# One 128-byte tensor ahead of the shared operand space in a two-block transformer kernel

## The chip, the core and the metric

The program runs on one NeuronCore of a Trainium2 chip. The metric is the device time of one execution in microseconds. The core has five engines with queues of their own: TensorE (PE, with its weight loads shown apart as PEld), VectorE (DVE), ScalarE (ACT), GpSimd (POOL) and SyncE (SP, which here only issues transfers).

## What is computed

Two blocks of two layers each work on x of 512 tokens by 2048 channels, in fp32. Each layer normalises x, multiplies it by a wide input matrix, mixes (gated linear attention and forgetting attention; a state space layer; a linear recurrent unit and window attention; latent attention and differential attention), gates, and multiplies by an output matrix:

```python
h = rms_norm(x, norm_g)
z = h @ w_in                     # 2048 x (4096 to 7200)
...                              # mixing and gates
return x + mixed @ w_out         # 2048 x 2048
```

The result is the normalised x after the fourth layer. The weight products are nearly all of the arithmetic.

## The kernel before

**Products.** Each large product runs in phases (the list PHASES), each phase in regions, blocks of 512 columns and pieces of 2 × 512 weights per partition. SP loads a piece into `raw` (a ring of four); ACT copies it to `whi`, rounded to fp32r (L386); DVE subtracts to make `wlo` (L392). The operand from x is split in the same way into `a_hi`, `a_lo` or `b_hi`, `b_lo`, each 16 tiles of 512 fp32r. TensorE then makes three products for each tile (L603):

```python
for n_pass, (ws, hs) in enumerate(((whi, hi), (whi, lo), (wlo, hi))):
    c = k * r.pitch
    if r.form == "T":
        lhsT = ws[:, slot, c + m * P:c + m * P + r.rows(m)]
        rhs = hs[:, kt, :]
    else:
        lhsT = hs[:, kt, m * P:(m + 1) * P]
        rhs = ws[:, slot, c:c + r.width]
```

In form "T" the weights are the stationary operand (loaded by LDWEIGHTS) and x is the moving one, 512 columns; in form "N" the roles change. Two regions have narrow stationary operands, of 24 and of 64 columns. Attention, recurrences and norms have small matmuls of their own, in plain fp32, which are put between the pieces.

**Order.** Each engine's instructions stand in a fixed order; `beside` and `mixed` deal the steps of a mixing stage out among the pieces of a product phase. Semaphores tie the engines together. L443 to L447 sum squares over the partitions with fp32 matmuls against `ones` and `eps_all`.

**Space.** `sb` places tensors one behind the other in each partition. First come those that live throughout. Everything else lies in one space behind them: `overlay(base, tensors)` lets groups of tensors share it, each group beginning `base` bytes (0, 65536 or 131072) behind the last tensor that `sb` placed. In the built program the addresses in bytes are:

```
raw    16512      acc       75744      a_hi, xa, w_p, d_ug   84864
whi    32896      eps_all   83040      r_y                   88992
wlo    49280      r_sp      84672      b_hi, xb, g_q, f_p   150400
stage  65664                           m_p                  176032
ident  73856      (r_sp is the         mx_o, glu_z          215936
ones   74368       last of sb)         s_kv ends at         228480
```

So `whi` begins at 128 modulo 256 and so does `a_hi`; from one to the other it is 51968 bytes, 203 times 256. `ones`, `ident`, `xa_acc`, `f_p` and `w_p` also are at 128 modulo 256, `acc` at 224, `eps_all` at 96, `m_p`, `m_o`, `r_y` and `r_o` at 160.

Of the kernel before, what the change touches and what calls it, by code (L numbers as in the profile page):

```python
# [127 lines left out]
def build(nc, inp, out):  # L128
    ctx = ExitStack()

    def sem(name):
        return ctx.enter_context(nc.semaphore(name))
# [4 lines left out]
    def sb(name, shape, dtype=F32):  # L137
        return ctx.enter_context(nc.sbuf_tensor(name, [P] + shape, dtype))
# [32 lines left out]
    eps_sq, eps_all, gains_two, rstd_col = sb("eps_sq", [1]), sb("eps_all", [P]), sb("gains_two", [KT]), sb("rstd_col", [NTOK])  # L171
    rows = sb("rows", [2, P])
    r_sp = sb("r_sp", [6, RB])
    ident_in = sem("identity_in")
    NCONST = len(VECTORS) + 3
    VECTORS_AFTER = 8
# [2630 lines left out]
```

## Time and profile before

| | |
|---|---|
| median of 3 runs | 3452.27 us (3450.07 to 3458.89) |
| profiled execution | 3455.26 us, its span 3453.5 us |
| mean granted TensorE clock | 0.988 |
| busy: PE, PEld | 3346.3 us (97%), 2702.4 us (78%) |
| busy: DVE, ACT, POOL | 1637.2 us (47%), 1289.0 us (37%), 520.9 us (15%) |
| moved by DMA | 525.06 MB, 152 GB/s |

The profiled execution takes 1.8 us more than its span from first to last instruction. Matmuls are pipelined: each is shown from its start to a modelled end, so that neighbours overlap; the pace of TensorE is read from one start to the next.

### The profile page before, as it was taken

The numbers are of one execution on the slowest core, as the hardware profiler recorded it, in microseconds if no ns is written. First come the engines' busy times: TensorE is split into PE (matmuls) and PEld (weight loads), VectorE is DVE, ScalarE is ACT, GpSimd is POOL, SyncE is SP. The second block draws the span as 40 slices with busy tenths as digits, with TensorE's granted clock in tenths as the row PEclk, the third lists the DMA queues.
The fourth block names the chain that finished last, engine by engine and source line by source line (L and its number), as shares of the span: only waits on it lengthen the run. The fifth ranks groups of instructions, "written<-read, shape, count | busy, mean of one in ns | idle before, by whom it ended". The sixth has DMA issues, their size and how long they took to land.

```text
span 3453.5 us, 41721 instructions
## 1 busy us (share of the span) xinstructions
PE 3346.3 (97%) x16417; PEld 2702.4 (78%) x16417; DVE 1637.2 (47%) x2691; ACT 1289.0 (37%) x1997; POOL 520.9 (15%) x754
## 2 busy tenths in 40 slices
PE   7999999999999999999999899999999999999996
PEld 6777887888888888888887676788878788777885
DVE  7895654434344444344344655543324333455532
ACT  4443433343233333433342445433223333456322
POOL 0001312323110000100331010121000111110211
PEclk9999999999999999999999999999999999999998
DMA  6776433546348776544335343453434733433631
GB/s 208 217 234 195 129 104 111 157 141 215 121 169 218 220 216 171 183 146 145 119 108 177 107 132 105 143 193 119 146 85 130 217 120 107 138 116 107 215 129 68
DMA packets 278948, 525.06 MB, mean 152 GB/s; under 512 B 64126, under 2 KB 99525, under 8 KB 273633
## 3 DMA queue, kind: packets, MB, share of 16 engines
q1 hardware_dynamic: 222352, 336.59, 32.6%
q0 software_dynamic: 54224, 182.52, 15.5%
q10 hardware_dynamic: 2176, 3.28, 0.4%
q8 instruction: 131, 2.15, 0.3%
q14 instruction: 65, 0.52, 0.0%
HBM read 408.32 MB, written 113.97 MB: 151 GB/s over the span
## 4 chain that ended last, share of the span: by engine, by line
PE 70%; DVE 4%; ACT 3%; DMA 2%; issue 2%; POOL 1%; ACTq 0%; DVEq 0%; POOLq 0%
PE pg L603 61%; PE pm L1288 2%; PE pm L1317 2%; DMA mx_g<-zt 2%; PE pm L1304 1%; PE pm L2392 1%; ACT whi L386 1%; PE pm L2396 0%; PE pm L2380 0%; DVE r_y L1673 0%; DVE d_x L2480 0%; ACT stage L481 0%; DVE xa L699 0%; ACT w_p L1353 0%; POOL mx_o L850 0%
## 5 line engine op out<-in xcount | busy, mean ns | idle before, releaser
L392 DVE TENSOR_TENSOR wlo<-raw,whi 128x1024 fp32r<-128x1024 f32 x523 | 664.3, 1275 | 1253.9 <-ACT whi L386 1253.0
L386 ACT ACTIVATE whi<-raw 128x1024 fp32r<-128x1024 f32 x523 | 548.6, 1054 | 1103.7 <-PE pg L603 1103.2
L603 PE MATMUL pg<-a_hi,whi 128*128 128x512 f32 x1856 | 744.3, 401 | 11.6 <-DVE wlo L392 4.3
L603 PE MATMUL pg<-a_hi,wlo 128*128 128x512 f32 x1856 | 727.2, 392 | 0.0
L603 PE MATMUL pg<-a_lo,whi 128*128 128x512 f32 x1856 | 726.4, 391 | 0.0
L603 PE MATMUL pg<-b_hi,whi 128*128 128x512 f32 x1568 | 618.9, 395 | 8.9 <-DVE stage L546 3.2
L603 PE MATMUL pg<-b_hi,wlo 128*128 128x512 f32 x1568 | 611.5, 390 | 0.0
L603 PE MATMUL pg<-b_lo,whi 128*128 128x512 f32 x1568 | 611.0, 390 | 0.0
L603 PEld LDWEIGHTS pg<-a_hi,whi 128*128 128x128 f32 x1856 | 348.5, 188 | 91.0 <-issue 14.3
L603 PEld LDWEIGHTS pg<-a_hi,wlo 128*128 128x128 f32 x1856 | 348.3, 188 | 77.9
L603 PEld LDWEIGHTS pg<-a_lo,whi 128*128 128x128 f32 x1856 | 348.9, 188 | 73.6 <-issue 2.6
L603 PEld LDWEIGHTS pg<-b_hi,whi 128*128 128x128 f32 x1568 | 294.8, 188 | 75.1 <-issue 6.5
L603 PEld LDWEIGHTS pg<-b_hi,wlo 128*128 128x128 f32 x1568 | 294.7, 188 | 62.4
L603 PEld LDWEIGHTS pg<-b_lo,whi 128*128 128x128 f32 x1568 | 294.8, 188 | 60.5 <-issue 1.2
L645 POOL DMA_DIRECT2D zt<-stage x144 | 78.5, 547 | 573.4 <-DVE stage L546 291.6
L603 PE MATMUL pg<-whi,a_hi 128*128 128x512 f32 x384 | 155.9, 406 | 0.0
L603 PE MATMUL pg<-wlo,a_hi 128*128 128x512 f32 x384 | 150.3, 391 | 0.0
L603 PE MATMUL pg<-whi,a_lo 128*128 128x512 f32 x384 | 149.9, 390 | 0.0
L1353 ACT ACTIVATE m_p<-m_p,m_small 128x128 f32<-128x128 f32 (+3 forms) x96 | 54.1, 563 | 211.0 <-DVE m_small L1419 210.5
L1416 DVE CUSTOM_DVE_ANT_0 m_p<-pm,wide 128x128 f32<-128x128 f32 (+3 forms) x96 | 47.1, 491 | 138.8 <-PE pm L1288 69.6
L657 POOL TENSOR_TENSOR acc<-acc,xa_sq 128x512 f32<-128x512 f32 x45 | 62.2, 1383 | 307.3 <-ACT xa_sq L505 302.1
L603 PE MATMUL pg<-whi,b_hi 128*128 128x512 f32 x256 | 101.7, 397 | 0.0
(434 smaller groups left out, 3844.8 us busy)
## 6 DMA issues: line engine op xcount, KB each, us to landing
raw<-in_l_w_in SPq DMA_DIRECT2D x169, 512.0 KB, 3.7
raw<-in_ab_w_in SPq DMA_DIRECT2D x112, 512.0 KB, 3.7
zt<-stage POOLq DMA_DIRECT2D x142, 256.0 KB, 3.6
raw<-in_c_w_in SPq DMA_DIRECT2D x64, 512.0 KB, 5.0
raw<-in_l_w_out SPq DMA_DIRECT2D x64, 512.0 KB, 3.7
raw<-in_ab_w_out SPq DMA_DIRECT2D x32, 512.0 KB, 3.7
raw<-in_glu_w SPq DMA_DIRECT2D x32, 512.0 KB, 4.4
raw<-in_c_w_out SPq DMA_DIRECT2D x32, 512.0 KB, 3.7
```

Of the source, the lines that this page charges most:

```text
L386: nc.scalar.activation(used(whi, n), used(raw, n), ACT.Copy).then_inc(hi_ready, 1)
L392: nc.vector.tensor_tensor(used(wlo, n), used(raw, n), used(whi, n).bitcast(F32), ALU.subtract).then_inc(lo_ready, 1)
L603: ins = nc.tensor.matmul(pg[m][:r.rows(m), :r.cols()], lhsT, rhs, start=(kt == 0 and n_pass == 0), stop=(kt == r.kts - 1 and n_pass == 2))
L645: pool.dma_start(r.dst(i, m, r), stage[:r.rows(m), m, :r.cols()]).then_inc(stored[m], 16)
L657: nc.gpsimd.tensor_tensor(total[:, :], total[:, :], squares[:, m % 2, :], ALU.add).then_inc(acc_done, 1)
L1288: ins = nc.tensor.matmul(pm[n % 2][:, :count * P], lhsT, rhs, start=(i == 0), stop=(i == len(ops) - 1))
L1304: ins = nc.tensor.transpose(pm[2][:, at:at + P], p[:, b * P:(b + 1) * P], ident[:, :])
L1317: ins = nc.tensor.matmul(pm[3][o * a.dv:(o + 1) * a.dv, qb * P:(qb + 1) * P], a.value(t, o, first + b), a.buf["pt"][:, n % 2, at:at + P], ...
L1353: nc.scalar.activation(p, p, ACT.Exp, bias=a.buf["small"][:, s:s + 1], accum_out=a.buf["small"][:, 4 + s:5 + s]).then_inc(att["probs"], 1)
L1416: run(vec.tensor_tensor_reduce(out=a.buf["p"][:, s, :count * P], in0=pm[n % 2][:, :count * P], in1=a.bias(t, qb, count), scale=a.scale, sc ...
L2392: nc.tensor.matmul(y_of(j), V6["d_x"][:, n, j, :, :].rearrange("p g k -> p (g k)"), V6["d_C"][:, n, j, 1:, :], start=(n == 0 and j % 4 == ...
```

## The change

One tensor of 32 floats, 128 bytes in each partition, is placed behind `r_sp`. Nothing reads or writes it. No instruction is added, removed or moved. Every tensor of `overlay` begins 128 bytes later; `raw`, `whi`, `wlo`, `stage`, `ident`, `ones`, `cols`, `acc`, `rstd` and the other tensors of `sb` stay. `a_hi` then begins at 84992, a multiple of 1024, and lies 52096 bytes behind `whi`, which is 203.5 times 256. The last byte used moves from 228480 to 228608.

```diff
@@ -171,6 +171,7 @@
     eps_sq, eps_all, gains_two, rstd_col = sb("eps_sq", [1]), sb("eps_all", [P]), sb("gains_two", [KT]), sb("rstd_col", [NTOK])
     rows = sb("rows", [2, P])
     r_sp = sb("r_sp", [6, RB])
+    sb("space_ahead_of_operands", [32])
     ident_in = sem("identity_in")
     NCONST = len(VECTORS) + 3
     VECTORS_AFTER = 8
```

## Rows read from the trace of the kernel before

**Rows 1.** The page: the span, and the chain that ended last, by engine and line.

```profile
span 3453.5 us, 41721 instructions
...
PE 70%; DVE 4%; ACT 3%; DMA 2%; issue 2%; POOL 1%; ACTq 0%; DVEq 0%; POOLq 0%
PE pg L603 61%; PE pm L1288 2%; PE pm L1317 2%; DMA mx_g<-zt 2%; PE pm L1304 1%; PE pm L2392 1%; ACT whi L386 1%; PE pm L2396 0%; PE pm L2380 0%; DVE r_y L1673 0%; DVE d_x L2480 0%; ACT stage L481 0%; DVE xa L699 0%; ACT w_p L1353 0%; POOL mx_o L850 0%
```

**Rows 2.** The page's costliest groups: the products of L603, first of three passes.

```profile
L603 PE MATMUL pg<-a_hi,whi 128*128 128x512 f32 x1856 | 744.3, 401 | 11.6 <-DVE wlo L392 4.3
...
L603 PE MATMUL pg<-b_hi,whi 128*128 128x512 f32 x1568 | 618.9, 395 | 8.9 <-DVE stage L546 3.2
...
L603 PE MATMUL pg<-whi,a_hi 128*128 128x512 f32 x384 | 155.9, 406 | 0.0
...
L603 PE MATMUL pg<-whi,b_hi 128*128 128x512 f32 x256 | 101.7, 397 | 0.0
```

**Rows 3.** Timeline, form T: start us, us, engine, what.

```profile
1650.17 0.39 PE L603 MATMUL pg<-b_hi,whi 128*128 128x512 f32 x1
1650.17 0.19 PEld L603 LDWEIGHTS pg<-b_lo,whi 128*128 128x128 f32 x1
...
1650.39 0.39 PE L603 MATMUL pg<-b_lo,whi 128*128 128x512 f32 x1
```

**Rows 4.** Chain that ended last, in order of time: start us, us, instructions.

```profile
1022.36 32.79 PE pg L603 x144
...
1064.00 16.55 PE pg L603 x72
...
1388.23 212.19 PE pg L603 x936
```

**Rows 5.** Timeline and busy table of a stretch at the lower clock.

```profile
532.28 0.63 PE L603 MATMUL pg<-whi,a_lo 128*128 128x512 f32 x1
532.71 0.63 PE L603 MATMUL pg<-wlo,a_hi 128*128 128x512 f32 x1
533.13 0.44 PE L603 MATMUL pg<-whi,a_hi 128*128 128x512 f32 x1
...
529.90:533.20 3.30, 3.19 (x12) 2.93 (x13) 2.90 (x4) 1.54 (x3) 3.21 (x3) 0.50 0.71 212
1388.00:1600.00 212.00, 212.00 (x938) 175.56 (x936) 86.19 (x97) 74.86 (x91) 29.21 (x54) 1.00 0.51 166
```

**Rows 6.** Timeline of the sums of squares, plain fp32.

```profile
1792.97 1.02 PE L443 MATMUL pm<-xa_acc,ones 128*128 128x512 f32 x2
1793.82 1.02 PE L444 MATMUL pm<-acc,eps_all 128*128 128x512 f32 x2
1794.68 1.02 PE L445 MATMUL pm<-acc,ones 128*128 128x512 f32 x2
```

**Rows 7.** Timeline of the two narrow regions, first and last of eleven and nine.

```profile
85.60 0.40 PE L603 MATMUL pg<-a_hi,wlo 128*24 128x512 f32 x1
...
87.92 0.40 PE L603 MATMUL pg<-a_hi,whi 128*24 128x512 f32 x1
...
2540.15 0.40 PE L603 MATMUL pg<-a_hi,whi 128*64 128x512 f32 x1
...
2542.00 0.39 PE L603 MATMUL pg<-a_hi,wlo 128*64 128x512 f32 x1
```

**Rows 8.** Groups of instructions, shapes apart: same shape, other addresses.

```profile
L1353 ACT ACTIVATE w_p<-w_p,w_small 128x256 f32<-128x256 f32 x48 | 24.5, 509 | 1.6
...
L1353 ACT ACTIVATE m_p<-m_p,m_small 128x256 f32<-128x256 f32 x24 | 12.2, 510 | 41.4 <-DVE m_small L1419 41.4
```

**Rows 9.** DMA issues: KB each, median us from issue to landing.

```profile
mx_g<-zt POOLq DMA_DIRECT2D x48, 256.0 KB, 4.2
...
mix<-r_o POOLq DMA_DIRECT2D x8, 256.0 KB, 2.3
...
mix<-w_o POOLq DMA_DIRECT2D x8, 256.0 KB, 2.3
```

## The prediction

> **What bounds the kernel now.** I read the chain that ended last first: TensorE holds 70% of it, L603 alone 61%, transfers 2% [rows 1]. Then the costliest groups: L603 runs 3 × (1856 + 1568 + 384 + 256) = 12,192 matmuls of 512 columns on the two operand pairs, and their idle time before is some 20 us in all [rows 2]. So TensorE is almost never starved, and what counts is its pace. The timeline gives it: a matmul starts 0.22 to 0.23 us after the one before, its weight load starts with the matmul ahead of it and is over after 0.19 us [rows 3]. Over a long stretch the pace is sharper: 936 matmuls in 212.19 us, 226.7 ns each, at the full granted clock (1.00, the 2.4 GHz level) [rows 4, 5]. 12,192 × 226.7 ns = 2764 us, 80% of the span.
>
> Within those 226.7 ns there is something to ask about. In a stretch with the granted clock at 0.50 (1.2 GHz) three starts lie 0.85 us apart, 425 ns a matmul [rows 5]. Half of that is 212.5 ns, so at the higher clock each matmul takes 226.7 - 212.5 = 14.2 ns more than a doubling of the pace would give. If those 14.2 ns came from where the operands lie, the change could touch 12,192 × 14.2 ns = 173 us.
>
> **The change, part by part.** It adds no instruction, no transfer, no wait and no semaphore, and each queue keeps its order. SP's and POOL's queues are past nothing new. What it alters is one relation: the stationary and the moving operand of L603 were both at 128 modulo 256 bytes; now the weights are there and the x operand is at 0. The work is the same, so every term is the duration of something at another address.
>
> *TensorE.* The direct row is the sums of squares: three fp32 products of 512 columns, back to back. L443 reads operands 0 bytes apart modulo 256 (`xa_acc` and `ones`), L444 operands 128 bytes apart modulo 256 (`acc` and `eps_all`), L445 96 bytes apart. They start 0.85 and 0.86 us apart and each lasts 1.02 us [rows 6]. The relation that the change makes is the one of L444, and it costs nothing there. They are plain fp32 and spend 0.85 us on 512 columns where fp32r spends 0.227, so a conflict could hide in them that shows at four times the pace. That is what stays unknown.
>
> Two more rows bear on the fp32r pace itself. In form N the operands change roles: moving is `whi` at 128 modulo 2048, stationary is `b_hi` at 896 modulo 2048 plus steps of 512; 144 matmuls take 32.79 us, 227.7 ns [rows 4]. In form T it is the other way round, at 226.7. So differences in the higher bits of the address do nothing. And where the stationary operand is only 24 or 64 columns, so that far fewer bytes of weights are read, the pace is (87.92 - 85.60)/10 = 232 ns and (2542.00 - 2540.15)/8 = 231 ns [rows 7], not less. If reads of weights stole time from the reads of the moving operand, fewer weights would steal less. The extra 14.2 ns so look like something each fp32r matmul pays at the higher clock, wherever its operands are. I take 0 us. The bounds: -173 us if all of it goes, and, as nothing excludes a loss, +173 us if as much again comes.
>
> The Trainium skill, TensorE: Matmul & The Clock Gate, section "Wait — 56ns, not 53.3ns?", gives N ÷ 2.4 GHz plus about 2.5 ns from start to start, 215.7 ns at 512 columns. The trace has 226.7 for fp32r. By the page, 12,192 × 11.0 ns = 134 us would be there to win, if layout were the cause; the page doesn't say that it is, and no run here shows it.
>
> *Contention.* Not every stretch runs at 226.7: one of 72 matmuls takes 16.55 us, 229.9 ns [rows 4], while other engines work beside it. If the new addresses removed or brought such stretching on every matmul, that would be 12,192 × 3.2 ns = 39 us either way. I take 0, as the same set of engines reads and writes the same amounts.
>
> *ACT, DVE, POOL.* Their operands move by 128 bytes too. Same work at other addresses costs the same: L1353 on 128x256 takes 509 ns on `w_p` (128 modulo 256) and 510 ns on `m_p` (160) [rows 8]. They also lie beside TensorE's work most of the time: 4% and 3% of the chain [rows 1]. Were a DVE or ACT operation on the chain 1% slower, that would be 0.07 × 3453 × 0.01 = 2.4 us. I take 0.
>
> *Transfers.* Loads of weights and stores from `stage` keep their addresses. Those into and out of the shared space move from 128 to 0 modulo 256. Stores of the same size from `w_o` (128) and `r_o` (160) land after the same 2.3 us [rows 9]. On the chain transfers are 2%, mostly `mx_g`, whose 256 KB take 4.2 us [rows 1, 9]. Were each of them 5% shorter, 0.02 × 3453 × 0.05 = 3.5 us would go; I take 0 and keep 3.5 us as the bound either way. The Trainium skill, DMA: Bandwidth & Descriptors, section "How a descriptor splits into AXI transactions", has a transfer that does not start on a multiple of 256 bytes fetch the bytes below its start too. A run of 2048 bytes that starts 128 bytes off would cost 68 beats against 64; by it an estimate is 6% off the transfers on the chain, 4 us, which is not to be seen here either.
>
> **Sum.** 0 + 0 + 0 + 0: the profiled time of 3455.3 us stays. The three runs have a median of 3452.3 us, 3.0 us below the profiled execution, so I forecast 3452 us. About what a measurement can tell from no change is 0.3%, 10.4 us; that is 10.4 us / 12,192 = 0.85 ns on each matmul.
>
> **The rivals.**
>
> *The phase of the operands is what costs the 14.2 ns* (faster). For it: both operands sit at the same place modulo 256 in both forms and in every one of the 12,192, and all show the same pace, so the trace has no fp32r matmul that would refute it. Against it: the narrow weights, and L443 to L445 [rows 6, 7]. It would give 3452 - 173 = 3279 us. By the page on TensorE the pace would fall to 215.7 ns and the time to 3452 - 134 = 3318 us; the narrow regions don't agree with what it would need. Chance 0.06.
>
> *A new conflict between the two reads* (slower, the other side). The place: TensorE's reads at L603, where the weight load lies wholly inside the matmul before it [rows 3]. If equal phases are what keeps the two reads apart, unequal ones make them meet, at up to as much as is there now: 3452 + 173 = 3625 us. It decides from 0.85 ns a matmul. For it: nothing in the trace has fp32r operands half a 256-byte unit apart. Against it: L444 is such a pair and is not slower than L443, and the weight load has 0.03 us to spare in each pace [rows 3]. Chance 0.07.
>
> *Less contention with the other engines* (faster by a part of 39 us, 3414 to 3442 us): for it, the stretches at 229.9; against it, that most of the time is at 226.7 already, so only a part of the matmuls can gain. Chance 0.08. *More of it* (slower, 3462 to 3491 us): the same rows with the other sign. Chance 0.06.
>
> *The change doesn't do what it says*: the unused tensor might get no space, and all addresses would stay. That gives 3452 us as well and belongs to the forecast's case.
>
> **How the numbers follow.** No change that can be measured 0.73; faster 0.06 + 0.08 = 0.14; slower 0.07 + 0.06 = 0.13. The forecast's own range is 3442 to 3462 us. The two small cases reach to 3414 and 3491, but their whole price needs every matmul to be touched; with about the nearer two thirds of each, 3425 to 3480 us leaves under 2 in 10 outside. The large cases stay outside.
>
> **What would show it.** The pace of L603 in the long stretch beginning near 1388 us: 212.2 us for 936 matmuls if I am right. A total of 198 to 202 us would be the faster rival, over 213 the slower. The stretches of form N should show 227 to 228 ns, where now the weights' side is moving and x is stationary; if only one form changes, it is the moving operand's address that counts and not the relation. The narrow regions should stay at 231 to 232. ACT on 128x256 should stay at 510 ns, `mx_g` at about 4.2 us. The prediction is wrong if fp32r reads at full pace see a conflict that the four times slower fp32 pairs hide.

## The result, and the profile after

The changed kernel is slower: 3501.09 us median of 4 runs (3500.35 to 3501.86), against 3452.26 us median of 4 (3450.07 to 3458.89) before. The ratio is 1.0141, with a 95% interval of 1.0128 to 1.0153. The forecast of 3452 us was wrong, and so was its range, which ended at 3480 us.

The page of the changed kernel (the added line moves L603 to L604): the head, the chain that ended last by engine and line, and the costliest groups of the products.

```profile
span 3498.5 us, 41721 instructions
...
PE 3398.2 (97%) x16417; PEld 2703.0 (77%) x16417; DVE 1635.8 (47%) x2691; ACT 1289.5 (37%) x1997; POOL 519.7 (15%) x754
...
PE 87%; DVE 6%; ACT 4%; issue 2%; DMA 1%; POOL 0%; SPq 0%; ACTq 0%; DVEq 0%; POOLq 0%
...
L604 PE MATMUL pg<-a_hi,whi 128*128 128x512 f32 x1856 | 750.1, 404 | 11.8 <-DVE wlo L393 5.3
...
L604 PE MATMUL pg<-b_hi,whi 128*128 128x512 f32 x1568 | 627.3, 400 | 6.4 <-DVE stage L547 3.1
```

Against [rows 1, 2] the counts are the same, and the idle time before L604 has not grown. DVE, ACT and POOL are busy for the same time within 1.4 us. Only TensorE is busy for longer, 3398.2 against 3346.3 us. No new wait is to be seen; the same work takes longer. The shares of the chain, 87% here and 70% in [rows 1], can't be set side by side: the chain of the kernel before reaches back only to 594 us, this one to 3 us.

The chain in order of time shows by how much; columns are start, us and instructions.

```profile
1034.08 33.57 PE pg L604 x144
...
1076.59 16.93 PE pg L604 x72
...
1404.12 217.52 PE pg L604 x936
```

These answer to [rows 4]. The long stretch of form T has gone from 226.7 to 217.52 us / 936 = 232.4 ns a matmul, form N from 227.7 to 33.57 / 144 = 233.1 ns, and the stretch of 72 from 229.9 to 235.1 ns. So it is 5.2 to 5.7 ns on each in these stretches.

It is not the other engines. In both kernels the long stretch has an interval in which DVE, ACT and POOL do nothing. The busy table and the timeline, before:

```profile
1394.10:1399.90 5.80, 5.80 (x28) 4.79 (x27) 0.00 (x0) 0.00 (x0) 0.00 (x0) 1.00 0.77 238
...
1393.97 0.39 PE L603 MATMUL pg<-b_hi,wlo 128*128 128x512 f32 x1
...
1399.87 0.39 PE L603 MATMUL pg<-b_lo,whi 128*128 128x512 f32 x1
```

and after:

```profile
1410.00:1416.00 6.00, 6.00 (x27) 4.89 (x26) 0.00 (x0) 0.00 (x0) 0.00 (x0) 1.00 0.74 235
...
1409.99 0.40 PE L604 MATMUL pg<-b_hi,wlo 128*128 128x512 f32 x1
...
1415.81 0.39 PE L604 MATMUL pg<-b_hi,whi 128*128 128x512 f32 x1
```

From the first start to the last there are 26 matmuls before, 5.90 us or 226.9 ns each, and 25 after, 5.82 us or 232.8 ns each. The whole loss is there with the other three engines idle, at the same granted clock and nearly the same share of busy transfers (0.77 and 0.74). Nor is it the transfers. Over the whole traces, the matmuls of form T that start while the three engines are idle, and the transfers under a fifth busy in the 4 us around them, follow one another after 226.9 ns before (177 of them) and 232.4 ns after (170).

At the lower clock nothing is lost. Busy table and timeline after, answering to [rows 5]:

```profile
533.60:537.00 3.40, 3.40 (x13) 3.01 (x14) 2.75 (x5) 1.86 (x4) 3.17 (x2) 0.50 0.75 243
...
535.66 0.63 PE L604 MATMUL pg<-whi,a_lo 128*128 128x512 f32 x1
536.08 0.63 PE L604 MATMUL pg<-wlo,a_hi 128*128 128x512 f32 x1
536.51 0.63 PE L604 MATMUL pg<-whi,a_hi 128*128 128x512 f32 x1
536.94 0.43 PE L604 MATMUL pg<-whi,a_lo 128*128 128x512 f32 x1
```

1.28 us for three, 427 ns, where before it was 425. The 22 matmuls of this line that run at the lower clock in both kernels take the same time in sum, within 0.01 us. Nor is anything lost in plain fp32: the sums of squares, answering to [rows 6],

```profile
1818.79 1.02 PE L444 MATMUL pm<-xa_acc,ones 128*128 128x512 f32 x2
1819.65 1.02 PE L445 MATMUL pm<-acc,eps_all 128*128 128x512 f32 x2
1820.51 1.02 PE L446 MATMUL pm<-acc,ones 128*128 128x512 f32 x2
```

start 0.86 us apart, though `xa_acc` now lies 128 bytes off `ones` modulo 256. All 3756 matmuls outside this line that have the full clock in both kernels took 0.7 us less in sum. So of what this kernel does, only the fp32r products at the 2.4 GHz level feel the change.

**The account.** Both traces hold the same 16,417 matmuls in the same order, so that each step from one start to the next can be set against its like. The table sums up what the steps take more after the change.

| steps | number | after less before, us |
|---|---|---|
| L603, full width, full clock, under 350 ns | 12,368 | +62.5 |
| the same with a wait in them (over 350 ns) | 48 | -7.5 |
| L603 with 24 or 64 columns of weights | 96 | -0.1 |
| all other matmuls at the full clock | 3756 | -0.7 |
| at the lower clock in both | 62 | -0.2 |
| with another clock in one of the two | 86 | -9.0 |

The sum is 45.0 us, which is the difference of the spans, 3498.5 - 3453.5. The products lose 62.5 us / 12,368 = 5.1 ns each on average. Among them are those on the operands of latent attention, 408 in all, which the prediction's 12,192 left out. The average is under 5.7 ns because steps of form T with another engine at work beside them took 227.5 ns before against 226.9 without, and now take 232.6 and 232.5. Some 17 us come back. The steps with a wait in them are 7.5 us shorter, as is to be expected where TensorE arrives later at something that comes in its own time. And 9.0 us are the clock's: its mean is 0.991 after and 0.988 before. Why the clock fell less is not shown.

### The profile page after: what moved, and what is told of

Its sections match the earlier page's. It is cut to its first block, busy times and chain, and to the rows that moved or that the text cites. A ratio compares the mean times of both kernels' runs of the same rounds, so it can differ in the third digit from the quotient of the medians.

```text
span 3498.5 us, 41721 instructions
## 1 busy us (share of the span) xinstructions
PE 3398.2 (97%) x16417; PEld 2703.0 (77%) x16417; DVE 1635.8 (47%) x2691; ACT 1289.5 (37%) x1997; POOL 519.7 (15%) x754
## 4 chain that ended last, share of the span: by engine, by line
PE 87%; DVE 6%; ACT 4%; issue 2%; DMA 1%; POOL 0%; SPq 0%; ACTq 0%; DVEq 0%; POOLq 0%
PE pg L604 75%; PE pm L1289 2%; PE pm L1318 2%; PE pm L1305 1%; ACT whi L387 1%; PE pm L2393 1%; PE pm L1018 1%; DMA mx_g<-zt 0%; PE pm L2086 0%; PE pm L2397 0%; PE pm L2381 0%; DVE r_y L1674 0%; DVE xb_n L685 0%; DVE d_x L2481 0%; ACT stage L482 0%
## 5 line engine op out<-in xcount | busy, mean ns | idle before, releaser
L604 PE MATMUL pg<-a_hi,whi 128*128 128x512 f32 x1856 | 750.1, 404 | 11.8 <-DVE wlo L393 5.3
L604 PE MATMUL pg<-a_hi,wlo 128*128 128x512 f32 x1856 | 733.3, 395 | 0.0
L604 PE MATMUL pg<-a_lo,whi 128*128 128x512 f32 x1856 | 733.1, 395 | 0.0
L604 PE MATMUL pg<-b_hi,whi 128*128 128x512 f32 x1568 | 627.3, 400 | 6.4 <-DVE stage L547 3.1
L604 PE MATMUL pg<-b_hi,wlo 128*128 128x512 f32 x1568 | 620.0, 395 | 0.0
L604 PE MATMUL pg<-b_lo,whi 128*128 128x512 f32 x1568 | 619.8, 395 | 0.0
L604 PEld LDWEIGHTS pg<-a_hi,whi 128*128 128x128 f32 x1856 | 348.0, 188 | 98.7 <-issue 14.3
L604 PEld LDWEIGHTS pg<-a_hi,wlo 128*128 128x128 f32 x1856 | 347.5, 187 | 84.7
L604 PEld LDWEIGHTS pg<-a_lo,whi 128*128 128x128 f32 x1856 | 348.4, 188 | 80.7 <-issue 2.6
L604 PEld LDWEIGHTS pg<-b_hi,whi 128*128 128x128 f32 x1568 | 296.1, 189 | 78.7 <-DVE wlo L393 5.8
L604 PEld LDWEIGHTS pg<-b_hi,wlo 128*128 128x128 f32 x1568 | 296.0, 189 | 69.6
L604 PEld LDWEIGHTS pg<-b_lo,whi 128*128 128x128 f32 x1568 | 296.3, 189 | 68.0 <-issue 1.2
L604 PE MATMUL pg<-whi,a_hi 128*128 128x512 f32 x384 | 157.5, 410 | 0.0
L604 PE MATMUL pg<-wlo,a_hi 128*128 128x512 f32 x384 | 151.8, 395 | 0.0
L604 PE MATMUL pg<-whi,a_lo 128*128 128x512 f32 x384 | 151.6, 395 | 0.0
L1354 ACT ACTIVATE m_p<-m_p,m_small 128x128 f32<-128x128 f32 (+3 forms) x96 | 54.1, 563 | 211.6 <-DVE m_small L1420 211.2
L604 PE MATMUL pg<-whi,b_hi 128*128 128x512 f32 x256 | 102.9, 402 | 0.0
```

What stands on the lines that cost most here:

```text
L604: ins = nc.tensor.matmul(pg[m][:r.rows(m), :r.cols()], lhsT, rhs, start=(kt == 0 and n_pass == 0), stop=(kt == r.kts - 1 and n_pass == 2))
L1354: nc.scalar.activation(p, p, ACT.Exp, bias=a.buf["small"][:, s:s + 1], accum_out=a.buf["small"][:, 4 + s:5 + s]).then_inc(att["probs"], 1)
```

## The experiments

Below, the distance is the start of the moving operand minus the start of the stationary one, modulo 256 bytes. In form T the moving operand is x, in form N it is the weights, so shifting x by d gives a distance of d in form T and of 256 - d in form N. The sizes are those of the chain's stretches, the times those of single runs unless an interval stands beside them; single runs of the kernel before, beside these, took 3447.4 to 3458.7 us.

**1. Is it the distance or the address?** One kernel has the unused tensor ahead of `whi` and not ahead of x:

```diff
+    sb("space_ahead_of_weights", [32])
     whi = sb("whi", [RING, PK * BLK], F32R)
```

> The unused 128 bytes stand ahead of whi and not ahead of the operands, so that whi, wlo, stage and all the shared space begin 128 bytes later: x lies at 0 modulo 256 as in the changed kernel, but the distance from the weights to x is the old multiple of 256. Theory D (the distance between the two operands of a product sets the pace of TensorE): 226.7 ns a matmul in the long stretch and about 3452 us. Theory A (the address of x itself, a multiple of 256, sets it): about 232.6 ns and 3500 us. Theory R (what matters lies between x and the tensors that stay, by way of other engines): raw alone has stayed, so about 3452 us unless it is raw, and then 3500 us.

Measured: 3448.35 us, beside 3451.59 us of the kernel before on the same chip. Theory D holds, theory A falls. Of theory R only the case of `raw` falls here; the rest of it falls in experiment 4, where `wlo128` moves `wlo` alone and most of the loss is there.

The second has both unused tensors.

> 128 unused bytes ahead of whi and 128 more ahead of the operands: x is back at 128 modulo 256, and the distance from the weights to x is 128 bytes off a multiple of 256. Theory D: about 232.6 ns a matmul and 3500 us, as in the changed kernel. Theory A: 226.7 ns and 3452 us. Theory R: 3500 us as well, since stage and the constants lie as far from x as in the changed kernel.

Measured: 3502.04 us. x is at its old place modulo 256 and all of the loss is there, with 232.4 ns in the long stretch. Theory A falls again.

```profile
1404.91 228.67 PE pg L605 x984
```

To have the first with an interval it was run once more.

> The kernel with the unused 128 bytes ahead of whi once more, timed against the kernel before. The distance from weights to x is as before and both lie 128 bytes later. If distance alone sets the time: within 0.3% of before, a ratio of 0.997 to 1.003, with x at a multiple of 256 as in the changed kernel. If the address of x has a part of its own in the 1.4%: over 1.003.

Measured: 3450.13 us median of 11 runs against 3452.22 us of 15, ratio 0.9994, interval 0.9985 to 1.0003. No change: x at a multiple of 256, as in the changed kernel, costs nothing when the weights go with it. Its chain has

```profile
1023.86 32.79 PE pg L604 x144
...
1389.72 223.07 PE pg L604 x984
```

which is 226.7 ns in form T and 227.7 in form N, as before.

**2. The period and the shape.** x is shifted by 256 and by 64 bytes (`[64]` and `[16]` in place of `[32]`).

> The unused tensor ahead of the operands is 256 bytes long. If the distance counts modulo 256 (or the address of x does): 226.7 ns a matmul and about 3452 us. If a longer period counts, 512 bytes or more: another pace, 228 ns or more and over 3465 us, or less than 226 ns.

Measured: 3452.20 us, and 212.20 us for the 936 matmuls. 256 bytes are as good as none.

```profile
1388.99 212.20 PE pg L604 x936
```

> The unused tensor ahead of the operands is 64 bytes long. If the pace is lost in proportion to the distance: about half of the loss, 229.7 ns and 3476 us. If any distance off a multiple of 256 loses it all: 232.6 ns and 3500 us. If only the bit of 128 bytes counts: 226.7 ns and 3452 us.

Measured: 3477.38 us, about half of the loss. But the chain shows that the forms part:

```profile
1030.25 33.70 PE pg L604 x144
...
1399.69 225.26 PE pg L604 x984
```

Form T, at distance 64, takes 228.9 ns; form N, at distance 192, takes 234.0. So the half is a mean over unlike paces, not a proportional loss, and the sign of the distance seems to count. That was tested by exchanging roles. Two shifts fit in one kernel if the second base of `overlay` is moved as well:

```diff
+    sb("space_ahead_of_operands", [48])
...
-    HALF = 2 * KT * L * 4
+    HALF = 2 * KT * L * 4 + 32
```

> Distances 192 (a) and 224 (b) in form T, 64 and 32 in form N. If the signed distance from stationary to moving operand is what counts, whichever of them is x: a in form T 233.3 ns as form N had with x 64 bytes later, a in form N 229 ns as form T had there, and about 3510 us. If it is the form that made form N slower at 64 bytes, form T stays near 229 to 230 ns at 192 and the time near 3480 us.

Measured: 3510.11 us. One run shows both forms with the same operands; before 461 us it is form T at distance 192, after 495 us form N at distance 64:

```profile
455.81 5.60 PE pg L604 x24
...
499.69 5.51 PE pg L604 x24
...
1036.88 33.70 PE pg L604 x144
...
1407.59 229.60 PE pg L604 x984
```

5.60 / 24 = 233.3 ns and 5.51 / 24 = 229.6 ns: within 0.7 ns the paces of `x64` with the forms exchanged. The signed distance decides here and not the form.

> Operands at base 0 (a_hi, a_lo) lie 32 bytes later than before and those at the second base (b_hi, b_lo) 96 bytes later, so that one run has four distances from stationary to moving operand modulo 256: 32 and 96 in form T, 224 and 160 in form N. Measured so far: 0 gives 226.7 ns, 64 gives 229, 128 gives 232.5, 192 gives 233.3. If the pace rises smoothly with the signed distance: 32 about 228 ns, 96 about 231 ns, 160 about 233 ns, 224 between 227 and 235 ns, and a time of 3475 to 3485 us. If only the size of the distance counted, 224 would equal 32 and 160 would equal 96.

Measured: 3515.73 us, well over what was expected. 32 bytes were expected to be nearly harmless and are not:

```profile
1038.17 33.84 PE pg L604 x144
...
1409.57 229.62 PE pg L604 x984
...
1846.05 67.32 PE pg L604 x288
```

The long stretch is at 233.4 ns: 768 of its 984 matmuls are on the a operands (distance 32), 216 on the b operands (distance 96), and both parts have this pace. The curve does not rise smoothly:

| distance | 0 | 32 | 64 | 96 | 128 | 160 | 192 | 224 |
|---|---|---|---|---|---|---|---|---|
| form T, ns | 226.7 | 233.4 | 228.9 | 233.8 | 232.4 | | 233.3 | 233.8 |
| form N, ns | 227.7 | 234.0 | 229.6 | | 233.1 | 235.0 | 234.0 | 233.3 |

(The values at 96 and 224 in form T are from the stretch of 288 matmuls on the b operands, 67.32 us in both runs, which in the kernel with x 256 bytes later takes 65.45 us, 227.3 ns. The form N values are from 144 matmuls, at 64 and 224 from 24, which take 5.60 us in `a32_b96` at 224. The two empty places were not measured.) Of the eight distances that of the kernel before is the best, with 64 in second place.

**3. Between the multiples of 32.** The x operands begin 16 or 8 bytes later inside tensors made longer by as much:

```diff
+    def split_at(name, base, floats):
+        whole = overlay(base, [(f"{name}_both", [2 * KT * L + floats], F32R)])[f"{name}_both"]
...
+    A, B = split_at("a", 0, 4), split_at("b", HALF, 60)
```

> Distances between the multiples of 32 tried so far: the a operands lie 16 bytes later than before and the b operands 240 bytes later (16 short of 256), in tensors made a little longer, all else at its old place modulo 256. Form T has 16 (a) and 240 (b), form N 240 and 16. Measured: 0 gives 226.7 ns, 32 and 224 give 233.2. If a distance near 0 leads the reads past one another as 0 does: 226 to 228 ns and about 3455 us. If only 0 and, less, 64 do: 232 to 234 ns and 3505 to 3515 us. A pace under 226 ns would show a better place than that of the kernel before and a time under 3440 us.

Measured: 3502.87 us. The long stretch takes 229.02 / 984 = 232.7 ns, but its parts differ. From start to start its 768 matmuls on a (distance 16) take 231.7 ns, its 216 on b (distance 240) 236.5 ns. Form N on b, at distance 16 like form T on a, takes only 227.6 ns:

```profile
1036.89 32.77 PE pg L609 x144
...
1405.77 229.02 PE pg L609 x984
...
1841.62 67.32 PE pg L609 x288
```

Here the forms part at one and the same distance, so the signed distance alone no longer tells the pace once one operand starts off a multiple of 32. Not even distance and form together do: the 288 matmuls of the last row are of form T at distance 240 too and take 233.8 ns, 2.7 ns less than those in the long stretch. Why is not shown.

> The same with 8 bytes: distances 8 and 248. If what meets is a unit of 16 bytes or more that both operands start in together: near 226.7 ns and about 3455 us for 8, while 248 may already be as slow as 224. If exact equality modulo 256 is needed: 232 to 234 ns in both and 3505 to 3515 us.

Measured: 3497.48 us. In the long stretch the a part (form T, distance 8) takes 233.3 ns, and form N at distance 8 takes 33.71 / 144 = 234.1 ns:

```profile
1034.23 33.71 PE pg L609 x144
...
1404.80 229.38 PE pg L609 x984
```

So 8 bytes are enough to lose it all in both forms; a shorter shift was not tried, and no place better than 0 was found.

**4. Which pair has to agree?** Each tile has the passes (whi, hi), (whi, lo), (wlo, hi). Tensors of one kind only were shifted by 128, all others kept modulo 256 by more unused space, as in

```diff
-    A = overlay(0, [("a_hi", [KT, L], F32R), ("a_lo", [KT, L], F32R)])
+    A = overlay(0, [("a_hi", [KT, L], F32R), ("space_ahead_of_a_lo", [32], F32), ("a_lo", [KT, L], F32R)])
```

> Only a_lo, b_lo and wlo lie 128 bytes later modulo 256; a_hi, b_hi and whi stay. The passes are (whi, hi), (whi, lo), (wlo, hi). Theory O (the stationary and the moving operand of the same matmul must agree): two of three matmuls have unlike operands, the pace goes to 229 to 232 ns and the time to 3480 to 3500 us. Theory N (a matmul's moving operand meets the weights that are loaded beneath it for the next one): in form T these pairs are hi with whi, lo with wlo, hi with whi, all of them alike, so that form T, 85% of the matmuls, stays at 226.7 to 227.5 ns and only form N slows; the time is 3452 to 3465 us.

Measured: 3491.86 us, form T at 227.44 / 984 = 231.1 ns. Theory N, by which form T would be untouched, falls. Theory O fits by the mean, but not by the pass: (whi, hi), whose own operands agree, takes 230.7 ns from its start to the next in form T, where 226.7 were to be expected.

```profile
1402.94 227.44 PE pg L605 x984
```

> Only a_lo and b_lo lie 128 bytes later modulo 256; a_hi, b_hi, whi and wlo stay as before. Theory O (a matmul's own two operands must agree): one of three matmuls is unlike in both forms, about 228.7 ns and 3477 us. Theory U (a matmul is slow where its moving operand disagrees with its own weights or with those loaded next beneath it): in form T only the second pass, 228.7 ns; in form N the first (whi moving, the x-lo tile loaded next) and the second, 230.6 ns; about 3480 us.

Measured: 3498.58 us, form T at 229.61 / 984 = 233.3 ns, form N at 33.39 / 144 = 231.9.

```profile
1033.57 33.39 PE pg L603 x144
...
1402.66 229.61 PE pg L603 x984
```

> Only wlo lies 128 bytes later modulo 256. Theory O: one of three in both forms, about 228.7 ns and 3477 us, the same as with the x-lo tiles alone. Theory U: in form T the second pass (x-lo moving, wlo loaded next) and the third (wlo its own weights), 230.6 ns; in form N the third alone, 228.7 ns; about 3496 us.

Measured: 3490.47 us, form T at 227.44 / 984 = 231.1 ns, form N at 231.9.

```profile
1033.58 33.39 PE pg L605 x144
...
1403.22 227.44 PE pg L605 x984
```

Theory O falls here: one unlike matmul in three costs far more than a third of 5.7 ns. The starts in the traces tell more, by pass. Each value is the mean from the start of that pass to the next start, on the a operands at the full clock:

| run, form | (whi, hi) | (whi, lo) | (wlo, hi) | what is odd |
|---|---|---|---|---|
| `wlo128`, T | 227.7 | 232.3 | 233.5 | stationary, third pass |
| `lo128`, N | 232.4 | 233.7 | 227.7 | stationary, second pass |
| `lo128`, T | 234.3 | 233.2 | 230.2 | moving, second pass |
| `wlo128`, N | 231.4 | 232.1 | 231.3 | moving, third pass |

With an odd stationary operand two passes are slow, the one that uses it and the one beneath which it is loaded, and the third is clean; that is what theory U says, in both forms. With an odd moving operand no pass is clean, and theory U falls: it has two clean passes in each of these two rows. Why the passes before and behind an odd moving operand are slow is not settled by this.

## Why the prediction was wrong

**The step that failed** is TensorE's term: "The relation that the change makes is the one of L444, and it costs nothing there ... I take 0 us." The term measured +62.5 us at the full clock, inside the bounds of ±173 us that stood beside it; with the 17 us that came back the change cost 45 us by the profiled times and 49 us by the medians. L444's row was read rightly, and L445 of the changed kernel repeats it at 0.86 us. But it is a plain fp32 product, which spends nearly four times as long on its columns. The text named this as the open point and then gave the row the weight of a refutation. Experiment 1 shows the opposite for fp32r: 128 bytes between the operands cost 1.4%, with x at 0 or at 128 modulo 256. The second argument, that a weight load has 0.03 us to spare in each pace, was none either: the loads last as long as before (PEld 2703.0 us against 2702.4), and the matmuls follow one another more slowly all the same.

**"So differences in the higher bits of the address do nothing"** was right: 256 bytes more changed nothing, and 227.7 in form N against 226.7 in form T was the same in each kernel at distance 0.

**The narrow regions** [rows 7] were argued to speak against a meeting of two reads. After the change they run at (88.20 - 85.90)/10 and (2580.08 - 2578.24)/8, 230 ns in both, where it was 232 and 231:

```profile
85.90 0.39 PE L604 MATMUL pg<-a_hi,wlo 128*24 128x512 f32 x1
...
88.20 0.39 PE L604 MATMUL pg<-a_hi,whi 128*24 128x512 f32 x1
...
2578.24 0.40 PE L604 MATMUL pg<-a_hi,whi 128*64 128x512 f32 x1
...
2580.08 0.40 PE L604 MATMUL pg<-a_hi,wlo 128*64 128x512 f32 x1
```

At distance 128 they lose nothing. That might suggest that a full weight load is needed for the loss, but the other runs speak against it. The region of 64 columns has 48 matmuls in a row; from the first start to the last it took (2550.96 - 2540.15)/47 = 230.0 ns before. In `wlo128` its first and last are

```profile
2569.55 0.40 PE L605 MATMUL pg<-a_hi,whi 128*64 128x512 f32 x1
...
2580.60 0.40 PE L605 MATMUL pg<-a_hi,wlo 128*64 128x512 f32 x1
```

which is 11.05/47 = 235.1 ns, and in `a16_b240` the same region takes 235.5 ns. So narrow loads do feel the place of the operands, though not when all three passes are 128 bytes off. The prediction's argument from [rows 7] can't be carried from one distance to another.

**The rival that came true** is "a new conflict between the two reads", with a chance of 0.07: right in place (L603's own two operands) and sign, and 5.1 ns a matmul where its full price was 14.2. That two reads meet stays an argument; what is shown is that the relation of the two addresses sets the pace. That the extra 14.2 ns over the doubled pace are owed to the layout is not borne out: none of the places tried went below 226.7 ns. It stays open where they come from.

**The other terms** of 0 hold (the lower end of the contention rival, 3452 - 39, is 3413 us and not 3414; nothing rests on it). ACT's L1354 on 128x256 takes 510 ns on `w_p` and `m_p`; `mx_g` lands after 4.0 us (4.2 before). Contention was no part of the loss either, by the interval with three idle engines. "The change doesn't do what it says" is out.

**Beside the pages.** The Trainium skill, SBUF — State Buffer, section "SBUF: two separate sides", says of the engine ports that "PE, ACT, and DVE's dedicated pair never wait on anyone". The loss is no such wait on another engine, as it is the same with the three others idle. But the sentence doesn't cover TensorE's own two operands, whose relation alone cost 5.9 ns a matmul in that interval. The estimate of 4 us less that the prediction made from the Trainium skill, DMA: Bandwidth & Descriptors, section "How a descriptor splits into AXI transactions", can be neither confirmed nor refuted: with x at a multiple of 256 and the distance kept, the timed pair gave 3450.13 against 3452.22 us, within the interval of no change.

## What to carry to other kernels

Where TensorE's pace in fp32r is the bound, look at the byte addresses of both operands, and let them begin at the same place modulo 256; an unused tensor ahead of one of them is enough to set it right, and a new small constant between them can lose over 1% without a single instruction changed, as it did here. Check it on the pace of a long stretch of the chain (here 226.7 against 232.4 ns), which tells it from one run. A row in another data type or at another rate doesn't stand in for the one that is missing: when it is the only evidence, the rival keeps its chance.

## What had not been expected of the hardware

The pace of fp32r matmuls of 512 columns depends on where their two operands start, modulo 256 bytes. At multiples of 32 the signed distance tells it, and not monotonically: in form T 226.7 ns at 0, 228.9 at 64, 232.4 at 128, and 233.3 to 233.8 at 32, 96, 192 and 224. Off the multiples of 32 the distance is not enough: 231.7 and 227.6 ns at 16 in the two forms, 236.5 and 233.8 ns at 240 in two stretches of one form. At the 1.2 GHz level and in plain fp32 the change cost nothing. With 64 columns of weights it cost nothing at distance 128, but 5 ns in two other runs. One odd operand in three passes slows passes whose own operands agree: with `lo` alone off, form T ran at 233.3 ns, above the 232.4 with all three passes off. How the reads meet inside the memory was not seen by any run.
